# Sixty-four unused bytes between the tiles of the split activations

## The reference

```python
h @ w_in                      # h: 512 or 256 tokens x 1024
a = jax.nn.relu(h @ w1)
(a * a) @ w2                  # the MLP, in four quarters of 1024 hidden features
y @ w_out
```

## Time and profile before

| | us |
|---|---|
| three runs | 1343.45, 1348.49, 1349.24 |
| median | 1348.49 |
| profiled execution, own time | 1348.33 |
| its span, first to last instruction | 1346.4 |
| around the span | 1.9 |
| TensorE busy | 1311.5 (97%) |
| VectorE busy | 988.9 (73%) |
| ScalarE busy | 668.7 (50%) |
| mean granted TensorE clock | 0.992 of full |

### The profile page before, as it was taken

The page is one execution under the profiler, slowest core; times in us unless marked ns, Lnnn a source line. Parts: engine busy times, 40 slices in busy tenths (PEclk is TensorE's granted clock), DMA queues, the critical chain, the costliest instruction groups (busy, mean ns, idle before and its releaser), DMA issues. The chain is left out here.

```text
span 1346.4 us, 25050 instructions
## 1 busy us (share of the span) xinstructions
PE 1311.5 (97%) x9434; PEld 1156.3 (86%) x9434; DVE 988.9 (73%) x1734; ACT 668.7 (50%) x1358; POOL 195.2 (14%) x268
## 2 busy tenths in 40 slices
PE   7999999999999999999999999999999999999997
PEld 6786679988888888898896899999999988999967
DVE  5698778999887878979428665655665786865974
ACT  4427743631523414334237664565465566465573
POOL 0101213000000000123104610000220016120043
PEclk8999999999999999999999999999999999999999
DMA  8774124365985867834320245655475433454511
GB/s 300 285 214 146 49 94 152 140 226 205 316 314 197 287 242 256 303 130 156 110 79 17 77 151 167 222 182 175 151 257 172 147 130 104 159 173 172 173 49 47
DMA packets 67665, 233.15 MB, mean 173 GB/s; under 512 B 7280, under 2 KB 12400, under 8 KB 67312
## 3 DMA queue, kind: packets, MB, share of 16 engines
q1 hardware_dynamic: 67568, 231.84, 50.2%
HBM read 230.76 MB, written 1.05 MB: 172 GB/s over the span
## 5 line engine op out<-in xcount | busy, mean ns | idle before, releaser
L957 DVE TENSOR_TENSOR wlo<-raw,whi 128x1024 fp32r<-128x1024 f32 (+1 forms) x284 | 346.4, 1221 | 148.5 <-ACT whi L599 142.7
L599 ACT ACTIVATE whi<-raw 128x1024 fp32r<-128x1024 f32 (+1 forms) x284 | 296.4, 1044 | 266.1 <-PE ps L1712 264.9
L1710 PE MATMUL ps<-Hh,whi 128*128 128x256 f32 (+1 forms) x896 | 302.6, 338 | 3.6 <-DVE wlo L957 1.6
L1711 PE MATMUL ps<-Hl,whi 128*128 128x256 f32 (+1 forms) x896 | 299.2, 334 | 0.0
L1712 PE MATMUL ps<-Hh,wlo 128*128 128x256 f32 (+1 forms) x896 | 298.9, 334 | 0.0
L1710 PEld LDWEIGHTS ps<-Hh,whi 128*128 128x128 f32 x896 | 169.2, 189 | 25.9 <-issue 5.7
L1712 PEld LDWEIGHTS ps<-Hh,wlo 128*128 128x128 f32 x896 | 169.0, 189 | 18.9
L1711 PEld LDWEIGHTS ps<-Hl,whi 128*128 128x128 f32 x896 | 169.4, 189 | 18.1
L1712 PE MATMUL ps<-HIDh,wlo 128*128 128x256 f32 (+1 forms) x536 | 176.1, 329 | 0.0
L1711 PE MATMUL ps<-HIDl,whi 128*128 128x256 f32 (+1 forms) x536 | 175.9, 328 | 0.0
L1710 PE MATMUL ps<-Gh,whi 128*128 128x256 f32 x624 | 175.6, 281 | 0.1
(11 more groups left out here) (266 smaller groups left out, 2061.5 us busy)
## 6 DMA issues: line engine op xcount, KB each, us to landing
raw<-wall SPq DMA_DIRECT2D x270, 512.0 KB, 4.2
aring<-aall SPq DMA_DIRECT2D x144, 512.0 KB, 4.7
raw<-wall SPq DMA_DIRECT2D x14, 384.0 KB, 3.0
AL<-ali SPq DMA_DIRECT2D x14, 192.0 KB, 5.5
X<-xin SPq DMA_DIRECT2D x2, 1024.0 KB, 7.1
BI<-rpb SPq DMA_DIRECT2D x4, 512.0 KB, 9.9
out<-X SPq DMA_DIRECT2D x4, 256.0 KB, 2.4
cst<-const SPq DMA_DIRECT2D x1, 960.0 KB, 8.4
```

The costliest lines, as they stand in the source:

```text
L599: act.activation(whi[:, slot, 0:n], raw[:, slot, 0:n], ACT.Copy).then_inc(sem("w_hi"), 1)
L957: dve.tensor_tensor(wlo[:, slot, 0:n], raw[:, slot, 0:n], whi[:, slot, 0:n].bitcast(F32), ALU.subtract)\
L1710: pe.matmul(o, a[0], b[0], start=first, stop=False)
L1711: pe.matmul(o, a[0], b[1], start=False, stop=False)
```

## The change

Six arrays get a row that is 16 floats (64 bytes) longer in each partition, and the program goes on using the first part of each row. The stride of `Hh`, `Hl`, `HIDh`, `HIDl` goes from 2048 to 2112 bytes, that of `Gh`, `Gl` from 1024 to 1088. `CQh` and `CQl`, the weights and everything else stay as they are. Each padded array is 8 x 64 = 512 bytes longer, so all arrays behind them move by multiples of 512 bytes.

```diff
-        Hh = sb("Hh", [P, KT, 2 * N], F32R, b1)
-        Hl = sb("Hl", [P, KT, 2 * N], F32R, b1)
+        Hh = sb("Hh", [P, KT, 2 * N + 16], F32R, b1)[:, :, 0:2 * N]
+        Hl = sb("Hl", [P, KT, 2 * N + 16], F32R, b1)[:, :, 0:2 * N]
...
-        HIDh = sb("HIDh", [P, KT, 2 * N], F32R, sm)
-        HIDl = sb("HIDl", [P, KT, 2 * N], F32R, sm)
+        HIDh = sb("HIDh", [P, KT, 2 * N + 16], F32R, sm)[:, :, 0:2 * N]
+        HIDl = sb("HIDl", [P, KT, 2 * N + 16], F32R, sm)[:, :, 0:2 * N]
...
-        Gh = sb("Gh", [P, KT, N], F32R, b2)
-        Gl = sb("Gl", [P, KT, N], F32R, b2)
+        Gh = sb("Gh", [P, KT, N + 16], F32R, b2)[:, :, 0:N]
+        Gl = sb("Gl", [P, KT, N + 16], F32R, b2)[:, :, 0:N]
```

## The result

The padded kernel is **slower by 0.55%**: a median of 1353.48 us over nine runs (1351.57 to 1354.43) against 1345.19 us over nine runs of the kernel before (1343.30 to 1349.24). The ratio is 1.0055, with an interval from 1.0042 to 1.0067. The forecast was 1345.5 us and no change; the time lies inside the range of 1325 to 1359, on the side that had 0.24. The profiled execution took 1353.56 us, 5.2 us more than the profiled one of before, which was itself among the higher of its runs; so the traces show 5.2 of the 8.3 us between the medians. The mean granted clock of the two profiled executions was 0.992 before and 0.995 after, so a lower clock is not the reason.

A forecast was written before the change was run, and what follows sets the result against it. TensorE's own matmul pace was taken as the bound. From 1348.33 us, -1.2 us (512-wide) and -1.6 us (256-wide), other terms 0, in all -2.8 us, gave 1345.5 us; range 1325 to 1359 us.

The forecast's parts named there:

- What bounds the kernel: Whole kernel: TensorE, busy 97% of the span and never fed too late; the pace of its own matmuls sets the time.
- Issued work: Whole kernel: no instruction, wait or DMA is added or moved and no queue changes its order; cost 0.
- writers: Writes into the padded arrays, such as ScalarE's 634 ns copy: the destination's address costs nothing; taken as 0.
- placement: Arrays behind the padded ones: they move by multiples of 512 bytes, so their remainders stay; cost 0.
- The 512-wide moving reads: TensorE's 512-wide matmuls: 1248 of H gain 2.2 ns each, 696 hidden ones lose 2.2 ns; sum -1.2 us.
- The 256-wide moving reads: TensorE's 5208 256-wide matmuls: -0.3 ns each, taken between two ways of averaging; -1.6 us.
- mean by levels: 256-wide matmuls: the mean of 117.8 and 113.4 ns, 115.6 against 116.7 now; -1.1 ns each.
- mean by distances: 256-wide matmuls: H and G 116.0 ns, hidden and `values` 117.8, mean 117.2; +0.5 ns each.
- The rival on the slower side: TensorE's sums: changing distances break the low level's rhythm, +5.7 us at 256 wide, +3.1 at 512; 1357.1 us; chance 0.24.
- The faster rival: TensorE's matmuls: low levels everywhere, -5.5 us and -17.2 us, 1325.6 us; faster rivals 0.36, of which 0.04 much faster.
- Nothing: TensorE's pace depends on something else, such as where arrays lie as a whole; 1348.3 us; shares 0.40 with the forecast.
- The sign of being wrong: Profile after: 512-wide distances clearly under 226 or over 236 ns would mean the unseen distances decide, not those averaged.

## Why the prediction was wrong, step by step

**What bounds the kernel** was right: TensorE has no new wait, and the whole difference is its pace.

**Issued work, writers, placement**, each costed at nothing, were right: equal counts, 632 ns for the copy, and a pad that keeps the distances leaves the levels of HID and G where they were.

**The 512-wide moving reads** were right in direction and nearly in size. The two half quarters met at 44.50 us (44.4 forecast), and the sum is -0.7 us (-1.2 forecast), or +0.3 without the shorter pauses. This was in part luck: 231.1 was the mean of two prices, the mean of all eight is 230.5, and the change runs at 231.8.

**The 256-wide moving reads** are the step that failed. The prediction took a mean by levels and a mean by distances as the two ways to average, put -0.3 ns between them, and had -1.6 us; the trace shows +6.3 us, and +8.4 by pace alone. Both ways averaged levels that had been seen at 448 and 320, odd multiples of 64. Four of the eight distances to come are even multiples, and at constant distance those cost 118.6 to 120.0 ns. Their mean is 119.3; with the other four at 117.8 that makes (119.3 + 117.8)/2 = 118.5, and the change runs at 118.0 to 118.4. This takes the odd ones at their high level, and a large part of the loss lies there: of the some 1500 matmuls near 113.3 (1300 in the prediction) none is left in a long stretch, and lifting them to 117.8 would alone cost 1500 x 4.5 = 6.7 us. The even distances are what turned the sum: with odd ones that change, the 256-wide paces come to -0.4 us against before, with even ones to +10.4, with all eight to +8.4. How the loss divides between the low level gone and the dear distances is not shown. The prediction said that for the other six distances it has no row, and then let the bounds come "from the observed levels". The bound above should have been open.

**The rival on the slower side** came nearest: its +8.8 us stand against 8.3 between the medians, and it had the right signs in the profile: 281 everywhere and no stretch of 113.4. Its mechanism, that changing the distance breaks the good rhythm, is borne out in part: in the sums of G and H the stretches at 113.3 are gone in every kernel whose distances change by other than 256 bytes, with odd distances alone too, and come back where G keeps its distance. But `values` holds the low level through changing odd distances, and the whole kernel loses nothing with them (0.9988), against 0.67% with even ones. The clause at its end, "or where the six unseen distances are worse than the two known", is what happened as well. Its other part, the hidden 512-wide rising to 233.3, was too much: 231.8.

**The faster rival** needed distances better than those of before. They exist for 512 columns, 0 and 256, but a spread over all eight buys the dear ones with them. Chosen instead of spread, they give 1335.39 us, about half of the way from 1344.72 to that rival's 1325.6.

**"Nothing"**, that the pace depends on where arrays lie as a whole, fell with the constant distances: moved by 64 bytes, H went from 233.3 to 226.7 ns and HID from 228.9 to 233.3.

**The sign of being wrong** did not show clearly: it watched the 512-wide ones for distances under 226 or over 236 ns. They ran at 231.8 and 231.9 in the mean, and of their single distances 46 of 1944 lie at 237 to 241. It was set on the part that held; no such sign was set for the 256-wide ones, where the loss came.

The Trainium skill (SBUF — State Buffer, section Who interferes with whom) calls TensorE's read ports for the moving operand and for weight loads independent. By that, as the prediction read it, the time would have stayed at 1348.3 us. These runs disagree: the distance between the two reads makes 6.6 ns of 226.7.

## What to carry to other kernels

Where TensorE is the bound, take its pace from the starts in the timeline, array by array and width by width. If equal shapes run at different paces, shift whole arrays by a few unused bytes at constant stride and price each distance to the stationary operand, before spreading over all of them: a spread takes in the dear distances with the good ones, and here it also lost the low level. Then choose for each width by itself, since in this kernel the distances that were best for 512 columns were the worst for 256.

## What the runs showed of the hardware that was not expected

- With split operands, TensorE's pace depends on the distance between moving tile and weight block: 226.7 to 233.3 ns for 512 columns, 113.3 to 120.0 for 256, nearly repeating after 256 bytes. It does so whichever of the two the activation is: `values` went from 117.8 to 120.0 with H at 0. Whether that is a conflict of the two reads in memory was not shown; the runs show the dependence alone.
- At odd multiples of 64, 256 columns have two levels on the same addresses, 113.3 and 117.8, each kept over long stretches; at 128 there were 118.6 and 120.0, at 0, 256 and 384 only one was seen. What decides which level a stretch takes was not found. That it lies behind the wider spread of the kernel before (5.9 us over nine runs, against 2.9 after the change) is argued, not shown.
- When distances change inside a sum, 512 columns do not run at the mean of the constant prices: 231.8 against 230.5 with all eight, 230.2 against 231.1 with odd ones, 232 against 229.8 with even ones. Nor do 256 columns: G ran at 117.8 with changing even distances, under all their prices. Why is open.
